# Attention scores of both components issued alternately on the two row halves, masks last, one maximum for both

## The reference

```python
q = apply_rope(rms_norm(q.reshape(B, Lp, N_HEADS, 2, HEAD_DIM), q_norm[l]), cos, sin)
k = apply_rope(rms_norm(k.reshape(B, Lp, N_HEADS, 2, HEAD_DIM), k_norm[l]), cos, sin)
# diff_attention, per block of queries:
s = jnp.einsum('bqhcd,bkhcd->bchqk', qs, ks).astype(jnp.float32) * scale
s = jnp.where(mask, s, -jnp.inf)
p = jax.nn.softmax(s, axis=-1)
a = p[:, 0] - lam * p[:, 1]
outs.append(jnp.einsum('bhqk,bkhe->bqhe', a.astype(vs.dtype), vs))
```

## Time and profile before

| | |
|---|---|
| median of 3 runs | 2178.19 us (2176.39 to 2180.32) |
| the profiled execution's own time | 2175.55 us |
| span of the profiled execution | 2173.8 us |
| TensorE busy with matmuls | 1986.5 us, 91% |
| VectorE busy | 1439.8 us, 66% |
| ScalarE busy | 512.7 us, 24% |
| GpSimd busy | 1114.2 us, 51% |
| 64-row score products, 528 | 121.3 us |
| mean granted TensorE clock | 0.94 of full speed |

### The profile page before, as it was taken

The page is one execution under the profiler, slowest core; times in us unless marked ns, Lnnn a source line. Parts: engine busy times, 40 slices in busy tenths (PEclk is TensorE's granted clock), DMA queues, the critical chain, the costliest instruction groups (busy, mean ns, idle before and its releaser), DMA issues. The chain is left out here.

```text
span 2173.8 us, 34328 instructions
## 1 busy us (share of the span) xinstructions
PE 1986.5 (91%) x12902; PEld 1780.2 (82%) x12902; DVE 1439.8 (66%) x2118; ACT 512.7 (24%) x1697; POOL 1114.2 (51%) x884
## 2 busy tenths in 40 slices
PE   6887989989789999999998888899887899999999
PEld 5886878877789999999988787787766677888887
DVE  6889878779686444333467898887786664544443
ACT  2012434432341220101011123344223312201100
POOL 5556243232266766667655562333322676767664
PEclk9998898988799999999999998998889999999999
DMA  4212010111122222222232211111111222222222
GB/s 152 77 59 78 21 39 21 40 40 39 39 92 99 83 97 77 97 94 93 102 113 76 79 59 39 40 33 46 39 31 47 98 97 97 81 94 96 97 97 77
DMA packets 23869, 156.36 MB, mean 72 GB/s; under 512 B 2896, under 2 KB 3280, under 8 KB 6096
## 3 DMA queue, kind: packets, MB, share of 16 engines
q1 hardware_dynamic: 21744, 147.01, 19.3%
q10 hardware_dynamic: 2016, 7.86, 0.9%
HBM read 150.59 MB, written 4.26 MB: 71 GB/s over the span
## 5 line engine op out<-in xcount | busy, mean ns | idle before, releaser
L559 PE MATMUL psum<-u,w_hi 128*128 128x264 f32 (+1 forms) x4480 | 934.3, 321 | 68.4 <-DVE glu_g L1229 19.1
L559 PEld LDWEIGHTS psum<-u,w_hi 128*128 128x128 f32 x4480 | 698.7, 194 | 129.0 <-issue 39.1
L475 POOL TENSOR_TENSOR w_lo<-w_raw,w_hi 128x512 fp32r<-128x512 f32 x544 | 761.9, 1430 | 11.3
L559 PE MATMUL psum<-u,w_lo 128*128 128x264 f32 (+1 forms) x2240 | 577.6, 319 | 0.0
L472 POOL TENSOR_TENSOR tick<-ones 128x1 f32<-128x1 f32 x136 | 30.8, 226 | 738.0 <-PE psum L559 632.6
L559 PEld LDWEIGHTS psum<-u,w_lo 128*128 128x128 f32 x2240 | 377.0, 194 | 25.7
L607 PE MATMUL psum<-w_hi,u 128*128 128x256 f32 (+1 forms) x1856 | 367.2, 300 | 10.9 <-issue 10.9
L428 DVE SCALAR_TENSOR_TENSOR psum<-xg,pvec,psum 128x512 f32<-128x512 f32 x440 | 332.4, 755 | 30.7 <-DVE psum L428 15.2
L607 PEld LDWEIGHTS psum<-w_hi,u 128*128 128x128 f32 (+1 forms) x1856 | 288.7, 187 | 20.8 <-issue 11.7
L607 PE MATMUL psum<-w_lo,u 128*128 128x256 f32 (+1 forms) x928 | 273.8, 295 | 0.0
L473 POOL TENSOR_SCALAR w_hi<-w_raw 128x2048 fp32r<-128x2048 f32 x136 | 261.9, 1926 | 0.0
(11 more groups left out here) (160 smaller groups left out, 2172.0 us busy)
## 6 DMA issues: line engine op xcount, KB each, us to landing
w_raw<-w_slabs SPq DMA_DIRECT2D x136, 1024.0 KB, 4.8
h<-x_t SPq DMA_DIRECT2D x4, 528.0 KB, 7.5
h<-x_t ACTq DMA_DIRECT2D x1, 2112.0 KB, 10.1
h_spill<-h ACTq DMA_DIRECT2D x8, 264.0 KB, 2.4
h<-h_spill ACTq DMA_DIRECT2D x1, 2112.0 KB, 11.4
out<-h SPq DMA_DIRECT2D x8, 256.0 KB, 2.0
rows<-rows ACTq DMA_DIRECT2D x2, 512.0 KB, 4.3
pvec<-pvecs ACTq DMA_DIRECT2D x2, 156.5 KB, 3.0
```

The source lines that it names most:

```text
L475: last = nc.gpsimd.tensor_tensor(w_lo[:, b, c:c + SLAB // 4], w_raw[:, b, c:c + SLAB // 4], w_hi[:, b, c:c + SLAB // 4], ALU.subtract)
L559: last = nc.tensor.matmul(psum[:, 2 * slot + j, 0:n], w[:, b, cut], src[:, part, kc, at0:at0 + n], start=(kc == 0 and m == 0), stop=(kc == ...
```

## The change

1. Scores are issued in steps, one for each group n of a head: both components' products alternate (c = 0 on rows 0 to 63, c = 1 on rows 64 to 127), into two neighbouring banks; the mask products of the group follow after all its products. Only three banks are used in all: even steps use banks S and S+1, odd ones S+1 and S+2.
2. A step waits until the exponentials of the first component in the step before are done (the one in the shared bank); ScalarE takes the component in the shared bank first.
3. A maximum covers both components at once, with nb announced once a step. The tail is first copied to SBUF (`s_tail`), and its exponentials read it there, in step 1.
4. In the lists of steps a head has three score steps where it had two passes, each behind its own tile: tile 5, 6 and 7 for h0, tile 8, 11 and 12 for h1 (before: 5 and 6, 8 and 11).
5. On VectorE the split of head 1's keys moves from behind the first maxima to before the seven (in the last stage eight) taps ahead of them; `maxima(h, 2)` is added right behind `maxima(h, 1)` (in the last stage with three taps or gate 5 between).

```diff
-    s = lambda h, c: [("s", h, c), ("e", h, c)]
+    s = lambda h, n: [("s", h, n), ("e", h, n)]
...
-        after = {..., 5: [("k", pair, 1)] + s(h0, 0), 6: s(h0, 1), 8: [("s", h1, 0)],
-                 9: [("t", h0, 0)], 10: [("t", h0, 1), ("e", h1, 0)], 11: [("pv", h0)] + s(h1, 1), 14: [("t", h1, 1), ("y", h0)]}
+        after = {..., 5: [("k", pair, 1)] + s(h0, 0), 6: s(h0, 1), 7: s(h0, 2), 8: [("s", h1, 0)],
+                 9: [("t", h0, 0)], 10: [("t", h0, 1), ("e", h1, 0)], 11: [("pv", h0)] + s(h1, 1), 12: s(h1, 2), 14: [("t", h1, 1), ("y", h0)]}
...
+                step = (layer * HEADS + hh) * 3 + n
+                banks = s_banks(step)
                 round_wait(pe, ROUND["k", layer, hh // 2, hh % 2])
+                if step:
+                    pe.wait_ge(exp_done, 2 * step - 1)
...
+                for k, (i, k0, k1, at0, m0) in enumerate(units):
                     t0, tn = TOK[i]
                     for m, (qp, kp) in enumerate([(0, 0), (0, 1), (1, 0)]):
+                        for c in range(2):
+                            rows64 = slice(HD * c, HD * c + HD)
+                            nc.tensor.matmul(psum[0:tn, banks[c], at0:at0 + k1 - k0], qk[rows64, 0, hh % 2, qp, t0:t0 + tn], qk[rows64, 1, hh % 2, kp, k0:k1],
+                                             start=(k == 0 and m == 0), stop=False)
+                for k, (i, k0, k1, at0, m0) in enumerate(units):
...
+                    for c in range(2):
+                        last = nc.tensor.matmul(psum[0:tn, banks[c], d0:d0 + dk], identb[0:tn, 0:tn], maskb[0:tn, m0:m0 + dk], start=False, stop=(k == len(units) - 1))
+                last.then_inc(s_full, 1)
...
+            def exps(layer, hh, n):
+                step = (layer * HEADS + hh) * 3 + n
+                act.wait_ge(max_ready, step + 1)
...
+                for c in (0, 1) if step % 2 else (1, 0):
+                    if n == 1:
+                        nc.scalar.activation(e[:, c, E_OFF[4] + FRONT:E_OFF[4] + T], s_tail[:, c, :], ACT.Exp, ...)
...
                     ins.then_inc(exp_done, 1)
...
+            def maxima(layer, hh, n):
+                step = (layer * HEADS + hh) * 3 + n
+                dve.wait_ge(s_full, step + 1)
+                for i in GROUPS[n]:
+                    if i == "tail":
+                        chain.mark(V.tensor_copy(s_tail[:], s_ps(step, i)))
+                        chain.mark(V.tensor_reduce(mx[:, :, 5], s_ps(step, i), AX_X, ALU.max))
+                    elif i in q_tiles(layer):
+                        chain.mark(V.tensor_reduce(mx[0:TOK[i][1], :, i], s_ps(step, i), AX_X, ALU.max))
...
                     qk_evict(layer, stage - 1, "k", 0)
+                    qk_evict(layer, stage - 1, "k", 1)
                     some_taps(8 if last else 7)
                     maxima(layer, h0, 0)
-                    qk_evict(layer, stage - 1, "k", 1)
                     if last:
                         gate(layer, 2)
                     some_taps(2)
                     maxima(layer, h0, 1)
                     if last:
                         some_taps(3)
+                    maxima(layer, h0, 2)
                     combine(layer, h0)
```

More of the change, by code:

```diff
@@ L79 @@
 E_N = 1360
-S_AT = {4: (0, 0), 3: (1, 0), 2: (2, 0), 1: (2, 272), 0: (2, 432)}
-S_TAIL = (2, 416)
+S_AT = {4: 0, 3: 0, 2: 0, 1: 272, 0: 432, "tail": 416}
 FRONT = 512
@@ L275, in build @@
         squares = at("squares", [P, 4, HD], F32, c); c += 4 * HD * 4
+        s_tail = at("s_tail", [P, 2, T - FRONT], F32, c); c += 2 * (T - FRONT) * 4
         assert c <= r_w
@@ L416, in st_ps, with s_banks, s_ps @@
             return psum[:, ST_BANK[0]:ST_BANK[k - 1] + 1:ST_BANK[1] - ST_BANK[0], 0:n // k]
+        def s_banks(step):
+            return S_BANK + step % 2, S_BANK + 1 + step % 2
+        def s_ps(step, i):
+            a, b = s_banks(step)
+            if i == "tail":
+                return psum[:, a:b + 1, S_AT[i]:S_AT[i] + T - FRONT]
+            return psum[0:TOK[i][1], a:b + 1, S_AT[i]:S_AT[i] + min(WIDTH[i], FRONT)]
         def conv_tap(layer, first, ch, k, begins, ends):
@@ L616, in t_round, with scores @@
                 return T_BANK + n % 2
-            def scores(layer, hh, c):
-                done = (layer * HEADS + hh) * 2 + c
+            def scores(layer, hh, n):
+                step = (layer * HEADS + hh) * 3 + n
+                banks = s_banks(step)
                 round_wait(pe, ROUND["k", layer, hh // 2, hh % 2])
-                rows64 = slice(HD * c, HD * c + HD)
-                def unit(i, k0, k1, bank, at0, m0):
+                if step:
+                    pe.wait_ge(exp_done, 2 * step - 1)
+                units = [(4, FRONT, T, S_AT[i], FRONT - TOK[4][0]) if i == "tail" else (i, 0, min(WIDTH[i], FRONT), S_AT[i], 0)
+                         for i in GROUPS[n] if i == "tail" or i in q_tiles(layer)]
+                for k, (i, k0, k1, at0, m0) in enumerate(units):
@@ L631, in unit @@
+                for k, (i, k0, k1, at0, m0) in enumerate(units):
+                    t0, tn = TOK[i]
                     dk = min(k1, WIDTH[i]) - max(k0, t0)
                     d0 = at0 + max(k0, t0) - k0
[L633 to L644, removed]
+                    for c in range(2):
+                        last = nc.tensor.matmul(psum[0:tn, banks[c], d0:d0 + dk], identb[0:tn, 0:tn], maskb[0:tn, m0:m0 + dk], start=False, stop=(k == len(units) - 1))
@@ L819, in b_evict @@
                     last.then_inc(b_free[n % 2], 1)
[L821 to L825, removed]
+            def exps(layer, hh, n):
+                step = (layer * HEADS + hh) * 3 + n
+                act.wait_ge(max_ready, step + 1)
+                if n == 0 and hh:
                     act.wait_ge(t_full, ROUND["p", layer, hh - 1, 3] + 1)
[L828 to L838, removed]
+                banks = s_banks(step)
+                for c in (0, 1) if step % 2 else (1, 0):
+                    x = hh % 2 * 2 + c
+                    if n == 1:
+                        nc.scalar.activation(e[:, c, E_OFF[4] + FRONT:E_OFF[4] + T], s_tail[:, c, :], ACT.Exp,
+                                             bias=nb[:, c, 4:5], scale=q_scale[:, 4, x:x + 1], accum_out=es[:, c, 5:6])
+                    for i in GROUPS[n]:
+                        if i in q_tiles(layer):
                             tn, w = TOK[i][1], min(WIDTH[i], FRONT)
-                            bank, at0 = S_AT[i]
-                            ins = nc.scalar.activation(e[0:tn, c, E_OFF[i]:E_OFF[i] + w], psum[0:tn, S_BANK + bank, at0:at0 + w], ACT.Exp,
+                            ins = nc.scalar.activation(e[0:tn, c, E_OFF[i]:E_OFF[i] + w], psum[0:tn, banks[c], S_AT[i]:S_AT[i] + w], ACT.Exp,
                                                        bias=nb[0:tn, c, i:i + 1], scale=q_scale[0:tn, i, x:x + 1], accum_out=es[0:tn, c, i:i + 1])
@@ L1090, in silu_lo @@
                 V.tensor_tensor(cact[:, 1, i, lo:lo + n], conv[:, i, lo:lo + n], cact[:, 0, i, lo:lo + n], ALU.subtract).then_inc(cact_ready, 1)
[L1092 to L1116, removed]
@@ new lines, in maxima @@
+            def maxima(layer, hh, n):
+                step = (layer * HEADS + hh) * 3 + n
+                dve.wait_ge(s_full, step + 1)
+                for i in GROUPS[n]:
+                    if i == "tail":
+                        chain.mark(V.tensor_copy(s_tail[:], s_ps(step, i)))
+                        chain.mark(V.tensor_reduce(mx[:, :, 5], s_ps(step, i), AX_X, ALU.max))
+                    elif i in q_tiles(layer):
+                        chain.mark(V.tensor_reduce(mx[0:TOK[i][1], :, i], s_ps(step, i), AX_X, ALU.max))
+                dve.wait_ge(v_chain, chain.value())
+                if n == 1:
+                    link(V.tensor_tensor(mx[:, :, 4], mx[:, :, 4], mx[:, :, 5], ALU.max))
+                j = (slice(0, 3), slice(4, 5), slice(3, 4))[n]
+                x = slice(hh % 2 * 2, hh % 2 * 2 + 2)
+                announce(dve, V.scalar_tensor_tensor(out=nb[:, :, j], in0=mx[:, :, j], scalar=-1.0,
+                                                     in1=q_scale[:, j, x].rearrange("p t c -> p c t"), op0=ALU.mult, op1=ALU.mult), max_ready, step + 1)
@@ L1328, in _ @@
                         gate(layer, 5)
+                        maxima(layer, h1, 2)
                         subln_stats(layer, h0)
```

8 lines of the change are left out of this document (3 added, 5 removed).

## The result

The changed kernel takes 2203.61 us (median of 4 runs, 2199.74 to 2206.96) against 2178.56 before: 1.0116 times as long, 95% interval 1.0103 to 1.0128, 25 us more. The forecast was 2197, slower, within 2160 to 2228. The profiled execution took 2199.74 us, 24.2 more than that of before (2175.55).

The account below looks back on a forecast made before the run. TensorE and VectorE were both taken as close to the bound, VectorE through waits in its program order. New waits and clock, less old waits and gains, gave layer 1 +16, layer 0 +3, last stages 0: +19 us, 2197, range 2160 to 2228.

Parts of the forecast that it names:

- TensorE's gain: Score products of both components at once on TensorE: 4.3 us per head against 8.1, 3.8 saved, 61 over 16 heads.
- VectorE's gain: Maxima of both components taken together on VectorE: 4.5 us a head against 5.3, 1.6 saved a stage.
- (a): VectorE idle before the split of head 1's keys, waiting for ScalarE's cast: 3.8 us in layer 1, 3.7 in layer 0.
- (b): Head 0, step 1: TensorE idles some 6 us before its products, and VectorE waits 0.9 to 1.2 us for them.
- the clock: Products after TensorE's 6 us idle run at half the granted clock: 2.1 us a stage, ends 0 and 4.
- (c): Head 0, between the maxima of steps 1 and 2, nothing else on VectorE: it idles 2.4 us.
- (d): After step 2's maxima, the subtraction of the weighted e awaits both components' exponentials: 1.7 us, against 1.9 to 2.5 before.
- (e): Second head, steps 1 and 2 back to back on VectorE: a wait of 2.4 us.
- GpSimd: Fewer VectorE operations meet GpSimd's split: 6, 6, 2 us back in layer 0 (step 0's scaling 1.2 worse), 0.7, 2.2, 0.7 in layer 1.
- The last stages: Each layer's shorter last attention stage, where long runs of taps partly cover the waits: +2 and -2 us, together 0.
- The rival without overlap: The halves do not overlap: 2.7 us more a stage, 16 in all, 2213, or 2227 with the split met; chance 0.15.
- The rival that TensorE decides: VectorE's waits shrink with the scores: six stages give up to 7.6 us each, 46 us, 2132 the end; chance 0.14.

## Why the prediction was right, point by point

**What bounds it.** Right: with TensorE at 97 to 99% the time still went up as TensorE's busy time fell by 73 us. One line of VectorE's order is worth more than the whole loss: with the split back the same change is 12 us faster than before. Moving the split alone in the old kernel (+63) shows that VectorE had no slack for it there either.

**TensorE's gain.** Forecast steps of 2.0 to 2.2, 1.15 and 1.0 us; measured 1.94, 1.17 (where the clock is full, in head 1) and 1.04. The unknown, whether the halves overlap, went as taken.

**VectorE's gain.** Forecast 1.6, 1.7 and 1.2 us for a head's maxima in layer 0; measured 1.57, 1.62 and 1.19.

**New waits.** (a) forecast 3.7 in layer 0 and 3.8 in layer 1, 2.8 in layer 0's first stage; measured 3.71, 3.73 and 3.13. (b) with the clock's share: forecast TensorE idle of some 6 us, measured 6.29; the wait at step 1 forecast 1.2 and 0.9, measured 2.1 and 1.8. (c) forecast 2.4, measured 3.2. (d) 1.7, measured 1.58. (e) 2.4, measured 2.57. The clock was booked apart at 2.1 a stage, 1.6 of it in head 0; (b) and (c) came 0.9 and 0.8 over, 1.7. With 0.2 over in (e) that term held in size. (a) to (e) and the clock were forecast at 12.7 to 13.6 us in the six stages and came to 12.6 to 14.2. One wait is in no term of the sum: the one at the next key statistics, 2.4, 0.8 and 1.9 us in layer 0 (before 1.3, 1.3 and 1.1) and 0.4 in layer 1. The old one was subtracted with the old waits, as if it would go.

**GpSimd.** The query statistics in layer 0 fell to 2.7 to 3.0 us as forecast, which is why the first two stages there came out even, and the scaling of head 1's step 0 rose to 1.09. The step that was missed: in layer 1 the weighted difference of head 0 now meets the split. Before and, below the dots, after:

```profile
1416.02 2.01 DVE L1130 SCALAR_TENSOR_TENSOR e<-e,er 128x144 f32<-128x144 f32 x4
...
1436.26 4.53 DVE L1128 SCALAR_TENSOR_TENSOR e<-e,er 128x144 f32<-128x144 f32 x4
```

That is 2.5 us more a stage, 7.6 in layer 1. The rest of VectorE's work there fell by 2.4 us more than forecast, and its idle time rose by 1.5 less.

**The sum.** Layer 1 came out at +19.9 against +16, layer 0 at +4.9 against +3: there VectorE's idle time came 2.5 us over, with the wait at the key statistics in it, and its busy time 1.0 under. The last stages were forecast at +2 and -2 and came at -0.8 and +2.6, each with the wrong sign; that they were booked as 0 together and gave 1.8 is luck. Outside the stretches nothing was to change. There 3.7 us came on top and 6.0 went, part of which is the chance of TensorE's clock behind layer 0's attention (32.2 us before, 28.5 after, see the masks behind each unit). So the mechanism and the parts of the full stages were right, and that the total lies within 7 us owes something to errors that offset each other. The six stretches were to be 57 to 60 us long and are 59.0 to 60.9.

**The upper end.** The rival without overlap was mis-sized: 16 us for it, 38 measured in one execution. At 2242 it lies above the range, which ended at 2228 and was meant to hold it with the split met besides. Its step 1 was priced at the full clock, though the same text had it run at the lower one.

**The rival that TensorE decides** asked for waits of VectorE under 9 us a stage. They were 13 to 16, the one at the key statistics included. With all taps spread by the traces they fall to 2 to 5 us, and the kernel is 2139 us, near the 2132 that the rival gave as its end. So the order written out for VectorE is what kept the change from it. That the gain is then the one the rival meant, TensorE's shorter scores, isn't shown, since the old kernel wasn't given that order.

## What to carry to other kernels

Where one engine is within a few per cent of full and a second fills its time with work and waits fixed in its own order, look at the order of the one that starts the round trips: a wait ahead of a long cover can cost more than itself. Here 3.7 us of wait cost 6 to 10 a stage in the old kernel, the lower clock after TensorE's idle included. When a change makes one pass into several dependent steps, list for each step what lies between its maxima and the next on the reading engine, and lay independent work there in the same edit. A wait blamed on an engine may be the tail of a chain that the waiting engine started; it then doesn't shrink when that engine comes later.

## What the runs showed of the hardware

- Products on rows 0 to 63 and on rows 64 to 127, in different banks, run at once without being issued alternately: three and three of 400 columns take 0.82 us either way (single half, three: 0.80). With twelve and twelve in a row step 0's products take 2.18 us against 1.35 alternated and 2.7 (1.35 and 1.33) one after the other; the second half's first product starts when three of the first half's are still to start. A single product over 128 rows between the halves ends the overlap (step 1: 1.62 and 1.64 us one after the other, 1.65 for both side by side).
- VectorE's operations on SBUF operands lose up to 1.7 us each while GpSimd splits: 1.91 us against 0.17 for one of 128x5, 1.19 against 0.18 for one of 128x20 (also for one with a single input, 344.97 above), 1.7 to 2.3 against 0.71 for those of 128x528. So a shift of a few us of VectorE against GpSimd changes what unchanged instructions cost.
- TensorE's granted clock differs between versions where no code differs: the same 28 products with v take 4.71 us in the change and 7.26 in the run with the masks behind each unit, in stretches of 28.5 and 33.2 us with mean granted clocks of 0.94 and 0.74. A difference of 5 us between two kernels can be this alone.
